# Sparse and latent attention with two heads to a unit, compressed keys of all heads at once, and the softmax division done by a diagonal in the turn

## What is computed

```python
def masked_softmax(s, mask):
    s = jnp.where(mask, s.astype(jnp.float32), NEG_INF)
    m = jnp.max(s, axis=-1, keepdims=True)
    p = jnp.where(mask, jnp.exp(s - m), 0.0)
    return p / jnp.maximum(jnp.sum(p, axis=-1, keepdims=True), TINY)
...
    o_c = jnp.einsum('bghqn,bngd->bqghd', p_c.astype(dt), v_cmp)
...
    return gb[..., 0:1] * o_c + gb[..., 1:2] * o_s + gb[..., 2:3] * o_w
```

## Time and profile before

| | us |
|---|---|
| median of 3 runs | 3315.85 |
| lowest, highest | 3314.59, 3319.35 |
| profiled execution | 3321.42 |
| its span | 3319.6 |
| mean granted TensorE clock | 0.91 |

### The profile page before, as it was taken

The page is one execution under the profiler, slowest core; times in us unless marked ns, Lnnn a source line. Parts: engine busy times, 40 slices in busy tenths (PEclk is TensorE's granted clock), DMA queues, the critical chain, the costliest instruction groups (busy, mean ns, idle before and its releaser), DMA issues. The chain is left out here.

```text
span 3319.6 us, 36522 instructions
## 1 busy us (share of the span) xinstructions
PE 2773.6 (84%) x13502; PEld 2103.2 (63%) x13502; DVE 1773.4 (53%) x2812; ACT 1309.8 (39%) x2034; POOL 234.8 (7%) x200
## 2 busy tenths in 40 slices
PE   3999867777999958977599959985799997977898
PEld 1766556556888837866433338863578786765686
DVE  2599767537999954356400035414555554157554
ACT  2223344335888843332211134412454443025543
POOL 1000034001101000023000000001000000020000
PEclk7999988888999978988699979997799999969999
DMA  5455400127996143210499954430144443400342
GB/s 220 178 215 216 178 1 1 51 84 268 412 411 266 52 158 127 81 48 1 163 352 412 406 188 178 186 124 5 51 177 190 161 186 125 182 1 1 150 184 78
DMA packets 94352, 536.70 MB, mean 162 GB/s; under 512 B 10849, under 2 KB 12257, under 8 KB 70625
## 3 DMA queue, kind: packets, MB, share of 16 engines
q1 hardware_dynamic: 87120, 508.41, 40.0%
q0 software_dynamic: 6768, 24.64, 2.1%
q10 hardware_dynamic: 288, 1.32, 0.1%
HBM read 599.87 MB, written 22.54 MB: 187 GB/s over the span
## 5 line engine op out<-in xcount | busy, mean ns | idle before, releaser
L1088 PE MATMUL ps<-w_hi,x_hi 128*128 128x512 f32 x1136 | 455.5, 401 | 14.1 <-DVE w_lo L2585 8.1
L1090 PE MATMUL ps<-w_hi,x_lo 128*128 128x512 f32 x1136 | 448.6, 395 | 0.0
L1089 PE MATMUL ps<-w_lo,x_hi 128*128 128x512 f32 x1136 | 448.1, 394 | 0.0
L1088 PEld LDWEIGHTS ps<-w_hi,x_hi 128*128 128x128 f32 x1136 | 217.3, 191 | 59.6 <-DVE w_lo L2585 8.5
L1088 PE MATMUL ps<-x_hi,w_hi 128*128 128x512 f32 (+1 forms) x512 | 203.9, 398 | 57.1 <-DVE x_lo L441 35.4
L1090 PEld LDWEIGHTS ps<-w_hi,x_lo 128*128 128x128 f32 x1136 | 216.7, 191 | 46.9
L1089 PEld LDWEIGHTS ps<-w_lo,x_hi 128*128 128x128 f32 x1136 | 217.5, 191 | 43.9
L1088 PE MATMUL ps<-w_hi,hidden_hi 128*128 128x512 f32 x536 | 210.8, 393 | 7.8 <-DVE hidden_lo L2752 6.0
L1090 PE MATMUL ps<-w_hi,hidden_lo 128*128 128x512 f32 x536 | 208.8, 390 | 0.0
L1089 PE MATMUL ps<-w_lo,hidden_hi 128*128 128x512 f32 x536 | 208.6, 389 | 0.0
L1089 PE MATMUL ps<-x_lo,w_hi 128*128 128x512 f32 (+1 forms) x512 | 196.8, 384 | 0.0
(11 more groups left out here) (615 smaller groups left out, 5791.8 us busy)
## 6 DMA issues: line engine op xcount, KB each, us to landing
weights_A<-in_moe_gate SPq DMA_DIRECT2D x132, 512.0 KB
weights_B<-in_moe_up SPq DMA_DIRECT2D x132, 512.0 KB
weights_A<-in_ffn_gu SPq DMA_DIRECT2D x24, 2048.0 KB, 7.4
weights_B<-in_ffn_gu SPq DMA_DIRECT2D x20, 2048.0 KB, 7.5
weights_C<-in_moe_down SPq DMA_DIRECT2D x66, 512.0 KB
weights_D<-in_moe_down SPq DMA_DIRECT2D x66, 512.0 KB
weights_C<-in_ffn_down SPq DMA_DIRECT2D x24, 1024.0 KB, 6.2
second_weights<-in_moe_gate SPq DMA_DIRECT2D x44, 512.0 KB
```

Source lines behind the costliest of these rows:

```text
L1088: nc.tensor.matmul(out, w_hi, x_hi, start=first, stop=False)
L1089: nc.tensor.matmul(out, w_hi, x_lo, start=False, stop=False)
L1090: return nc.tensor.matmul(out, w_lo, x_hi, start=False, stop=last)
```

## The change

- `attention` takes pairs: a unit is two heads a = 0, 1 and one query tile; 8 units in the latent stage, 16 in the sparse one. Scores of both heads go to two banks; the mask is two VectorE instructions (one a head) and the maximum one for both.
- In the sparse mixer each head's scores contract over its own 64 partitions, so they use the lower or the upper half of the array's rows, and the GpSimd masks of the queries go. The value products of the two heads alternate between the halves of the array's columns.
- The probabilities are no longer divided. VectorE makes one diagonal matrix per head and branch from identity and the gated reciprocal of the sum (`DG`), and the turn is a full product of probabilities and diagonal in place of a transpose.
- The compressed keys of all heads and both query tiles are scored in one run of 32 products between the first and the second unit's scores; their softmax is made once for all, turned four times, and each unit adds one product a head with a matrix `VB` that holds the compressed values in that head's 16 rows and zeros elsewhere.
- Two constants are new (136 columns), and the rows of the sparse output weights are in another order, done on the host.

```diff
-            PR = self.sb(ctx, "probs", [P, 2, width])
-            PT = self.sb(ctx, "probs_t", [P, 2, width])
...
+            PR = self.sb(ctx, "probs", [P, 2, 2, nb, SEQ])
+            PT = self.sb(ctx, "probs_t", [P, 2, 4 * nb * P])
+            DG = self.sb(ctx, "diagonals", [P, 2, 2 * nb, P])
...
                     def scores(u):
...
                         for b in range(nb):
-                            last = nc.tensor.matmul(ps[:, u % 2, b * SEQ:b * SEQ + W], q(h)[:, t * P:(t + 1) * P],
-                                                    keys(h)[:, b, 0:W], start=True, stop=True)
...
+                            for a in range(2):
+                                last = nc.tensor.matmul(score_bank(u, a)[:, b * SEQ:b * SEQ + W], queries(c, a)[:, t * P:(t + 1) * P],
+                                                        keys(c, a)[:, b, 0:W], start=True, stop=True)
...
+                    def compressed_scores():
+                        for t in range(2):
+                            for c in range(n):
+                                for a in range(2):
+                                    col = P * t + 16 * c
+                                    last = nc.tensor.matmul(ps[:, 7 - a, col:col + NC], queries(c, a)[:, t * P:(t + 1) * P],
+                                                            compressed[0](c, a), start=True, stop=True)
+                        last.then_inc(s["c_scores"], 1)
+                        nc.tensor.matmul(ps[:, 5, 0:SEQ], self.c("cmp_spread", P, p=NC), compressed[1],
+                                         start=True, stop=True).then_inc(s["v_spread"], 1)
...
-                            last = nc.tensor.transpose(ps[:, 4 + i // 4, (i % 4) * P:(i % 4 + 1) * P],
-                                                       PR[:, u % 2, col:col + P], self.c("ident"))
...
+                            last = nc.tensor.matmul(ps[:, 4 + i // 4, (i % 4) * P:(i % 4 + 1) * P], PR[:, u % 2, a, b, kt * P:(kt + 1) * P],
+                                                    DG[:, u % 2, a * nb + b, :], start=True, stop=True)
...
                     scores(0)
+                    if compressed:
+                        compressed_scores()
                     scores(1)
                     for u in range(N):
                         if u + 2 < N:
                             scores(u + 2)
                         transposes(u)
+                        if compressed and u == 0:
+                            compressed_turns()
                         if u >= 1:
                             product(u - 1)
...
-                        V.tensor_tensor(pr, pr, total[:, b2, 0:nb].unsqueeze(2).to_broadcast([P, nb, W]), ALU.mult).then_inc(s["scaled"], 1)
...
+                        V.tensor_tensor(DG[:, b2], self.c("ident").unsqueeze(1).to_broadcast([P, 2 * nb, P]),
+                                        tt.unsqueeze(2).to_broadcast([P, 2 * nb, P]), ALU.mult).then_inc(s["scaled"], 1)
+
+                    def compressed_max():
+                        dve.wait_ge(s["c_scores"], 1)
+                        for t in range(2):
+                            for a in range(2):
+                                sc = ps[:, 7 - a, t * P:(t + 1) * P].rearrange("p (c n) -> p c n", n=16)
+                                link(V.scalar_tensor_tensor(out=CP[:, t, 8 * a:8 * a + 8, 0:NC], in0=sc[:, :, 0:NC], scalar=scale,
...
                     mask_and_max(0)
+                    if compressed:
+                        compressed_max()
                     for u in range(N):
                         if u + 1 < N:
                             mask_and_max(u + 1)
                         normalise(u)
+                        if compressed and u == 0:
+                            compressed_shares()
+                            value_blocks()
...
-                    @block.gpsimd
-                    def _(pool):
-                        for h in range(16):
-                            g = h // 4
-                            nc.gpsimd.tensor_scalar(Q[:, h, :], QR[:, (g // 2) * 4 + h % 4, :], self.c("half", 1, off=g % 2), None,
-                                                    ALU.mult).then_inc(s["q_masked"], 1)
```

## The result

The changed kernel takes **3283.48 us** (median of 4 runs, 3279.47 to 3286.50) against 3316.74 for the kernel before beside it (4 runs, 3314.59 to 3319.35): ratio **0.9899, 95% interval 0.9881 to 0.9916**, 33 us less. The forecast was 29 less (3287; range 3272 to 3305). A second set of runs of the same kernel, the control of the second set of experiments, gave 3276.87 (3273.79 to 3283.03) and a ratio of 0.9879 (0.9857 to 0.9901). So two sets of runs of one kernel differ by 6.6 us, and a small difference between kernels of different sets says little.

A forecast was written before the change was run, and what follows sets the result against it. The prediction took a chain passing between engines, VectorE's work alternating with TensorE's turn, as the bound. Sparse stage -27, latent stage -2 and constants +0.2 gave -29 us, from 3315.85 to 3287 us, range 3272 to 3305.

The forecast's parts named there:

- The chain: Sparse stage: no engine is full; VectorE's next mask waits for TensorE's turn, 29 times, 28.4 us in all.
- The pair at full clock: Sparse steady part: two heads take 10.3 us, VectorE 6.9 plus turns 3.4, against 15.5 before.
- The pair at the low clock: Sparse steady part: turns 2.1 and 3.8 us, TensorE's own work 5.3 where 3.0 are covered; 15.1 per pair.
- The start: Sparse stage: third mask 20.5 us after the stage's first instruction, 12.9 later than before.
- two-sided bound: Sparse stage's 64 compressed-score instructions: 6.9 us if row halves run together, 13.8 if not; 6.9 taken.
- The sparse stage: Whole sparse attention: 20.5 + 78.4 + 6.6 = 105.5 us against 132.6, so -27.
- The latent stage: Latent attention: pairs of 8.0 us at clock 0.75, 34.9 us against 35.5; -2 taken.
- all full clock, 30.4: Latent attention: fast bound of 30.4 us (-5) if the clock is full throughout; all low would give 39 (+4).
- The second rival: Both attention stages: denser full products keep the clock high, all sparse pairs at 10.3, latent -5; 3274 us, chance 0.22.
- The third rival: Sparse stage: clock stays at 1.2 GHz, row halves run apart, TensorE bounds, pairs 16.8; 3340 us, chance 0.05.
- no change: Sparse stage: gain eaten by a 29 us start and pairs near 13.5; within 7 us of before, chance 0.06.
- The +0.2 for the larger constants: Kernel's beginning: TensorE's first instruction waits for constants grown by 136 columns; +0.2 us taken.

The follow-up runs named there:

- the kernel with full rows: Changed kernel with queries masked by GpSimd into full-row tiles and keys in full rows, so no product uses half the rows: 3287.0 us, ratio 0.9918.
- the filled kernel: Changed kernel with VectorE dividing, transposes, compressed work one unit later, plus idle TensorE matmuls ahead of each sparse turn: 3267.74 us, ratio 0.9862.

## Why the prediction came out right

- **The chain** (VectorE and the turn in alternation): right. In the changed kernel the mask waits for L2944 in all 13 units behind the third mask, and never for scores.
- **The pair at full clock**: forecast 10.3, measured 10.23 (waits 1.25 and 2.14 against 1.32 and 2.21). Each price in that sum was a row of before; only the linked start of a turn was 0.07 short. One place is misnamed: the 20 instructions of products and the scores of 256 columns stand behind the small tile's turn, ahead of the large one, and not behind the large tile's. The sum is not touched by it, since the 3.0 us of VectorE set against them are those of that place (from 2990.90 to 2993.71 below it is 2.8).
- **The pair at the low clock**: forecast 15.1. No pair ran wholly at the low clock; the slowest one of the control took 12.4 us at a mean of 0.72 (masks at 2984.78 and 2997.16):

```profile
2984.78 1.42 DVE L2997 SCALAR_TENSOR_TENSOR probs<-ps,constants 128x512 f32<-128x512 f32 x2 [2.31 <-PE ps L2944]
...
2990.90 0.88 DVE L2997 SCALAR_TENSOR_TENSOR probs<-ps,constants 128x256 f32<-128x256 f32 x2 [2.24 <-PE ps L2944]
...
2993.02 0.69 DVE L3017 TENSOR_TENSOR diagonals<-constants,total 128x512 f32<-128x512 f32 x1
2993.05 2.02 PE L2915 MATMUL ps<-nsa_k,nsa_q 64*128 64x256 f32 x8
...
2995.00 2.05 PE L2944 MATMUL ps<-diagonals,probs 128*128 128x128 f32 x16
...
2997.16 1.42 DVE L2997 SCALAR_TENSOR_TENSOR probs<-ps,constants 128x512 f32<-128x512 f32 x2 [3.45 <-PE ps L2944]
```

  The small turn ran at 0.50 and VectorE waited 2.24 for it (2.1 forecast). Then TensorE's other work, at 0.50 too, went on until 2995.00, while the diagonals were ready at 2993.71: it did outlast VectorE, as forecast, by 1.3 us. The 3.45 is this 1.3 and a large turn at full clock. A large turn at 0.50 stands at 2958.72 of the same trace: 3.78 us, and a wait of 3.94 (3.8 forecast). So the mechanism was right and one term too large: TensorE's other work took 4.3 us at the low clock (2990.72 to 2995.00) where 5.3 was taken, and outlasted by 1.3 where 2.3 was taken. With these numbers a pair at the low clock is an estimated 6.7 + 2.24 + 3.94 + 1.3 = 14.2. For the 13 units, six and a half pairs of 11.2, the forecast was 73; they took 68.3 in one execution and 74.1 in the other, by the clock.
- **The start**: forecast 20.5, measured 19.6 both times; the compressed scores 6.9, measured 6.88. The two-sided bound (6.9 or 13.8) was met at both ends, one by the changed kernel and one by the kernel with full rows (13.67). The Trainium skill (TensorE: Matmul & The Clock Gate, Part 3) says that weight loads overlap only where the row group differs; this pair of runs agrees, 0.1075 against 0.2136 us each. Its "only" the runs don't bear out: the value products of the two heads use all rows and alternate between column halves, and 16 of their instructions take 1.09 us (2977.14 of the changed kernel) where 8 in one half took 1.09 before (3004.62).
- **The sparse stage**: forecast 105.5, measured 101.5 and 104.8. The sum was good to 1 to 4 us. How near it comes within that is the clock's doing, which the prediction carried over from before (0.91) and which came out as 0.96 or 0.81.
- **The latent stage**: taken -2, measured -4.7 (and -5.6 in the control, 2331.76 to 2361.64). This term was mis-sized. Its pairs were to take 8.0 at a clock half low; the timeline of the changed kernel has them 6.33 us apart, a little under the 6.6 of full clock:

```profile
2335.82 0.62 DVE L2997 SCALAR_TENSOR_TENSOR probs<-ps,constants 128x128 f32<-128x128 f32 x2 [0.88 <-PE ps L2944]
...
2338.94 0.89 DVE L2997 SCALAR_TENSOR_TENSOR probs<-ps,constants 128x256 f32<-128x256 f32 x2 [1.32 <-PE ps L2944]
...
2342.15 0.62 DVE L2997 SCALAR_TENSOR_TENSOR probs<-ps,constants 128x128 f32<-128x128 f32 x2 [0.87 <-PE ps L2944]
...
2348.49 0.62 DVE L2997 SCALAR_TENSOR_TENSOR probs<-ps,constants 128x128 f32<-128x128 f32 x2 [0.87 <-PE ps L2944]
```

So the stage was nearly the "all full clock, 30.4" end of its bounds. The window's clock of 0.83 (0.75 before) means that what was low fell outside these pairs. The step that failed was to spread a stage's mean clock evenly over its units. That the clock rose at all had been taken from no row.
- **The second rival** (clock high, 3274): between it and the forecast lies what happened. One execution of the stage had 0.96 in its steady part, the other 0.81, against 0.90 before over the same stretch. The Trainium skill (TensorE: Matmul & The Clock Gate, Part 4) says that transposes don't count as activity for the clock. The runs leave that open. Over the 13 units the changed kernel had 0.96 and 0.81 with diagonals, 0.85 and 0.78 with transposes; with the compressed work later it was 0.85 and 0.81: both lean its way, the first by less than the spread. Without the compressed branch diagonals had 0.78 and transposes 0.85, and in the kernel before 0.88 and 0.90, which leans the other way.
- **The third rival** (slower, 3340) and "no change": the pairs never passed 12.4 us, where the third rival needed over 15 and "no change" 13.5, and the third mask came at 19.6, not at 29. The +0.2 for the larger constants is below what two executions differ by, and no run shows it.
- **What the prediction did not ask**: whether each part of the change gains. It priced the diagonals inside the pair and never wrote down the same pair with transposes. From the same rows that is VectorE 6.9 + 0.5 and turns of 0.8 and 1.25: 9.5, against 10.3, and 9.30 was measured. The step was there for the taking, and would have said that one of the three parts works against the others. The total came near its forecast without this question having been asked.

## What to carry to other kernels

- Where two engines hand one tile back and forth, moving work from one to the other gains only if it is cheaper there. Division inside a matmul sounds free, but an fp32 product is two instructions where a transpose is one, and in the kernel before alone it cost 18 us.
- Price each part of a compound change by itself: here pairs (-18) and the batched small branch (-19) paid for the diagonals (+8 here, +14 and +16 in two other kernels). A part's price depends on what it is taken out of.
- A tiny operand handled once for all heads beats sixteen times in a chain; put it where the chain has not yet filled, behind the second unit's scores and not ahead of them.

## What the runs showed of the hardware

- fp32 instructions with 128-column weights in alternating row halves run two at a time, 0.1075 us each at granted clock 0.50, against 0.2136 in full rows. The prediction had it as its likelier case, from column halves.
- One program gets different clocks in one stage from one execution to the next: 0.96 and 0.81 over the same 13 units, 5.8 us of a time of 3280. What decides it was not found.
- TensorE without a gap doesn't mean a high clock. It was busy for 27.0 us of 27.0 in the compression stage at 0.50, and again at 0.50 through the 13.6 us of compressed scores in full rows, while the filled kernel held 1.00. What the clock follows stays open: no run changed only that.
